# Feed-forward gate and up projections as seven block products in place of eight, with a six-place weight ring

## What is computed

```python
def swiglu(h, w_in, w_out):
    gt, up = jnp.split(h @ w_in, 2, axis=-1)       # w_in: 1024 x 5632
    return (jax.nn.silu(gt) * up) @ w_out          # w_out: 2816 x 1024
x = layer_norm(ALPHA * x + g1 * ox, ln_g[i, 0], ln_b[i, 0])
x = layer_norm(ALPHA * x + g2 * swiglu(x * (1.0 + sc2) + sh2, ...), ...)
```

## Time and profile before

| | us |
|---|---|
| median of 3 runs | 2932.16 (2931.82 to 2932.55) |
| the profiled execution: span from first to last instruction (no other time of it is given) | 2928.7 |
| TensorE busy | 2802.1 (96%) |
| VectorE / ScalarE / GpSimd busy | 1401.3 / 747.1 / 1211.0 |

### The profile page before, as it was taken

How to read it: one execution, slowest core, us unless ns; L and a number is a source line. 1 busy time by engine, 2 the same in 40 slices (tenths; PEclk the granted TensorE clock), 3 DMA queues, 4 the chain that set the end, 5 groups by cost and what they waited for, 6 DMA issues and landing times.

```text
span 2928.7 us, 38039 instructions
## 1 busy us (share of the span) xinstructions
PE 2802.1 (96%) x14458; PEld 2246.8 (77%) x14458; DVE 1401.3 (48%) x2147; ACT 747.1 (26%) x1218; POOL 1211.0 (41%) x583
## 2 busy tenths in 40 slices
PE   7899999999989899999997999999989999999997
PEld 2588888888867777777775888888778878888885
DVE  6433433334355466555556654645450045555555
ACT  3600000000034433333333222231441321222112
POOL 0544444444445321222221334433264366556555
PEclk9999999999999999999998999999999999999999
DMA  9211111111102010101010111112222311111113
GB/s 388 81 51 50 50 43 50 50 43 50 43 30 86 31 37 29 36 29 36 29 36 15 51 51 50 50 43 58 87 94 101 108 66 65 57 57 57 57 65 123
DMA packets 62900, 185.35 MB, mean 63 GB/s; under 512 B 17108, under 2 KB 23380, under 8 KB 60648
## 3 DMA queue, kind: packets, MB, share of 16 engines
q1 hardware_dynamic: 42016, 152.68, 15.3%
q10 hardware_dynamic: 20808, 31.61, 3.1%
HBM read 163.22 MB, written 21.05 MB: 63 GB/s over the span
## 4 chain that ended last, share of the span: by engine, by line
PE 86%; DVE 6%; ACT 3%; issue 3%; DMA 1%; POOL 1%; DVEq 0%; ACTq 0%; SPq 0%; POOLq 0%
PE ps L717 26%; PE ps L719 25%; PE ps L718 25%; PE ps L1057 2%; DVE acc L2197 1%; PE ps L785 1%; PE ps L1068 1%; DMA resid<-x_t 1%; PE ps L891 1%; PE ps L858 1%; PE ps L1414 1%; ACT sg_z L2000 1%; PE ps L1105 0%; PE ps L818 0%; DVE da_al L2368 0%
## 5 line engine op out<-in xcount | busy, mean ns | idle before, releaser
L540 POOL TENSOR_TENSOR slab_hi<-slab_raw,zero 128x1024 fp32r<-128x1024 f32 x227 | 446.4, 1967 | 1498.0 <-PE ps L719 1351.3
L717 PE MATMUL ps<-h_hi,slab_hi 128*128 128x512 f32 x2256 | 894.5, 397 | 12.5 <-POOL slab_lo L544 5.6
L718 PE MATMUL ps<-h_lo,slab_hi 128*128 128x512 f32 x2256 | 883.1, 391 | 0.0
L719 PE MATMUL ps<-h_hi,slab_lo 128*128 128x512 f32 x2256 | 883.1, 391 | 0.0
L544 POOL TENSOR_TENSOR slab_lo<-slab_raw,slab_hi 128x1024 fp32r<-128x1024 f32 x227 | 562.0, 2476 | 19.4 <-DVE mean L2251 1.7
L717 PEld LDWEIGHTS ps<-h_hi,slab_hi 128*128 128x128 f32 x2256 | 425.9, 189 | 112.6 <-issue 14.9
L719 PEld LDWEIGHTS ps<-h_hi,slab_lo 128*128 128x128 f32 x2256 | 425.6, 189 | 91.1
L718 PEld LDWEIGHTS ps<-h_lo,slab_hi 128*128 128x128 f32 x2256 | 426.0, 189 | 84.6
L2204 DVE TENSOR_TENSOR ffn_p<-ps,ffn_g 128x1024 f32<-128x1024 f32 x22 | 26.9, 1224 | 454.3 <-PE ps L719 448.7
L2197 DVE TENSOR_TENSOR acc<-ps,acc 128x512 f32<-128x512 f32 x352 | 228.2, 684 | 24.1 <-PE ps L719 22.9
L2195 DVE SCALAR_TENSOR_TENSOR resid<-ps,mod,resid 128x512 f32<-128x512 f32 x320 | 213.1, 743 | 0.0
(11 more groups left out here) (326 smaller groups left out, 4001.5 us busy)
## 6 DMA issues: line engine op xcount, KB each, us to landing
slab_raw<-w_in SPq DMA_DIRECT2D x168, 512.0 KB, 3.6
mod_big<-mod_w SPq DMA_DIRECT2D x12, 2048.0 KB, 11.7
slab_raw<-w_c SPq DMA_DIRECT2D x43, 512.0 KB, 3.6
res_scr<-resid ACTq DMA_DIRECT2D x4, 2048.0 KB, 7.2
resid<-res_scr ACTq DMA_DIRECT2D x2, 4096.0 KB, 12.3
gv_scr<-sg_t ACTq DMA_DIRECT2D x4, 2048.0 KB, 7.0
slab_raw<-gv_scr SPq DMA_DIRECT2D x16, 512.0 KB, 3.5
resid<-x_t SPq DMA_DIRECT2D x2, 2048.0 KB, 16.3
```

What stands on the lines that cost most here:

```text
L540: pool.tensor_tensor(hi, raw[slot][:], zeros, ALU.add).then_inc(hi_done.sem, 1)
L717: pe.matmul(dst, w_h, r_h, start=first, stop=False, skip_group_check=True)
L718: pe.matmul(dst, w_h, r_l, start=False, stop=False, skip_group_check=True)
L719: return pe.matmul(dst, w_l, r_h, start=False, stop=last, skip_group_check=True)
```

## The change

Per tile f = 1 to 21 the 2 x 2 product (gate, up) x (first, second half of k) times (first, second half of k) x (first, second half of the tokens) is made from seven block products (the Winograd form) in place of eight. A block product is 4 k x 3 = 12 matmuls over 512 tokens. Tile 0 stays as it was.

- Weights: of the four 128 x 512 blocks A11, A12 (gate), A21, A22 (up), GpSimd makes S1 = A21 + A22, S3 = A11 - A21, S2 = S1 - A11, S4 = A12 - S2 per tile (`weight_sums`). A11, S1, A12, S3, S4, S2, A22 and the two halves of w_out's slab then go, each as a high and a low part of 128 x 512, through a ring of six places (the three old slabs halved). All nine pairs are made on GpSimd.
- Inputs, once: four combinations T1 to T4 of h's four blocks, in float32, by GpSimd (T1) and VectorE (the rest); high parts on ScalarE, low parts on VectorE (12) and GpSimd (T3's four).
- Results: seven products in four banks (4 to 7), products accumulate in pairs where the sums allow it. ScalarE copies the first (`copy_first`) and the S1 product (`copy_fifth`) out of PSUM; VectorE makes four sums from PSUM and one from SBUF per tile, and the two products with the silu in halves.
- The residual's scaling by alpha moves from ScalarE to VectorE (`residual_in`). The output pass uses `PS[0]` and `PS[1]`, and waits for VectorE as before, four halves ahead.

```diff
 (GpSimd)
+def weight_sums(f):
+    for load in in_load: pool.wait_ge(load.sem, load.at(f))
+    a21 = block_source(S3)
+    pool.tensor_tensor(ffn_s1[:], a21, block_source(A22), ALU.add).then_inc(r_sum.sem, 1)
+    pool.wait_ge(r_sum.sem, r_sum.at(f, 0))
+    pool.tensor_tensor(a21, block_source(A11), a21, ALU.subtract).then_inc(r_sum.sem, 1)
+    pool.tensor_tensor(ffn_s2[:], ffn_s1[:], block_source(A11), ALU.subtract).then_inc(r_sum.sem, 1)
+    pool.wait_ge(r_sum.sem, r_sum.at(f, 2))
+    pool.tensor_tensor(ffn_s4[:], block_source(A12), ffn_s2[:], ALU.subtract).then_inc(r_sum.sem, 1)
+def ring_high(f, b, j):          # then block_high: wait for the sum or the load, 128x512 + zero
+    if j >= A22: pool.wait_ge(r_mm.sem, r_mm.at(f, j - A22))
+    elif j < S4: pool.wait_ge(r_mm.sem, r_mm.at(f - 1, j + 3))
+    else:        pool.wait_ge(f_om.sem, f_om.at(f - 2, (KT - 1, 2 * KT - 1)[j - S4]))
+def ring_turn(f, b):
+    for j in (A11, S1, A12, S3, S4, S2):
+        ring_high(f, b, j); block_low(f, b, j)
+    hidden_low(f - 1, 0)
+    for j in (A22, OUT_0, OUT_1):
+        ring_high(f, b, j); block_low(f, b, j)
+    weight_sums(f + 1)
+weight_sums(1)                   # the start, after h's low parts 1, 3, 5, 7
+for j in (A11, S1):
+    block_high(1, 0, j); block_low(1, 0, j)
+for k in range(2):
+    split_low(0, (KT + 2 * k + 1,)); input_difference(2 * k); input_difference(2 * k + 1)
+split_low(0, (2 * KT - 3, 2 * KT - 1))
 (TensorE)
+def ffn_in(f, b, first=False):
+    pe.wait_ge(f_silu.sem, f_silu.at(f - 1, 0));  ffn_product(f, b, A11)
+    pe.wait_ge(f_c.sem, f_c.at(f - 1, 0));        ffn_product(f, b, S1, (t_low, 0) if first else None)
+    pe.wait_ge(f_pc.sem, f_pc.at(f, 0));          ffn_product(f, b, A12)
+    pe.wait_ge(f_c.sem, f_c.at(f - 1, 2));        ffn_product(f, b, S3, (t3_low, 0) if first else None)
+    pe.wait_ge(f_pc.sem, f_pc.at(f, 1));          ffn_product(f, b, S4)
+    pe.wait_ge(f_u.sem, f_u.at(f - 1));           ffn_product(f, b, S2, (t_low, 4) if first else None)
+    pe.wait_ge(f_y.sem, f_y.at(f));               ffn_product(f, b, A22, (t_low, 8) if first else None)
 (VectorE)
+def ffn_upper(f):                # after product S3
+    dve.tensor_tensor(ffn_p5[:], BANK[7], ffn_p5[:], ALU.add)
+def ffn_hidden(f):               # after product S2, each with its waits
+    dve.tensor_tensor(ffn_u[:], BANK[5], ffn_p1[:], ALU.add)
+    dve.tensor_tensor(ffn_p1[:], BANK[6], ffn_u[:], ALU.add)
+    dve.tensor_tensor(ffn_p5[:], ffn_p5[:], ffn_u[:], ALU.add)
+    dve.tensor_tensor(ffn_c[:], BANK[7], ffn_u[:], ALU.add)        # after product A22
+    dve.tensor_tensor(ffn_c[:], ffn_c[:], ffn_g[:], ALU.mult)
+    dve.tensor_tensor(ffn_p5[:], ffn_p5[:], ffn_p1[:], ALU.mult)
+def ffn(f): ffn_upper(f); ffn_hidden(f); ffn_add_out(f - 1)
+# the start, in VectorE's order
+for k in half_k: turned_low(k, t1_lo[:, k, :], t1_raw[:, k, :], t1_hi[:, k, :])
+for k in half_k: input_fourth(k)
+for k in half_k: turned_low(KT + k, t2_lo[:, k, :], t2_raw[:, k, :], t2_hi[:, k, :])
+for k in half_k: turned_low(3 * KT // 2 + k, h_lo[:, k, HALF:T], t4_raw[:, k, :], h_hi[:, k, HALF:T])
+ffn_upper(1)
+dve.tensor_tensor(ffn_0[:], PS[1], ffn_0[:], ALU.mult)             # tile 0's hidden
+for k in range(KT): residual_in(k)                                # resid * ALPHA + res_b0, 128x1024
+ffn_hidden(1)
+ffn_add_out(0)
 (SP: slab 0 of f is loaded after the low part of A12 of f-1, slab 1 after A22's, slab C after OUT_1's)
```

More of the change, by code:

```diff
@@ L81, with ring_slot @@
 LAST_ON_POOL = KT + 5
+N_RING, N_BLOCKS, N_PROD = 6, 9, 7
+A11, S1, A12, S3, S4, S2, A22, OUT_0, OUT_1 = range(N_BLOCKS)
+LAST_F = F_TILES - 1
+FIRST_PAIR = IN_FFN_OUT - 2
+def ring_slot(b, j):
+    return (N_BLOCKS * b + j + 4) % N_RING
 DA_TILES = {3: (0, 1), 4: (2, 3), 5: (4, 5), 6: (6,), 7: (7,)}
@@ new lines, in _, with block_high @@
+            RING_SUM = {S1: 0, S3: 1, S2: 2, S4: 3}
+            def block_high(f, b, j):
+                if j in RING_SUM:
+                    pool.wait_ge(r_sum.sem, r_sum.at(f, RING_SUM[j]))
+                else:
+                    load, turn = {A11: (in_load[0], f), A12: (in_load[0], f), A22: (in_load[1], f)}.get(j, (c_load, f - 1))
+                    pool.wait_ge(load.sem, load.at(turn))
+                pool.tensor_tensor(ring(all_hi, b, j).rearrange("p k f -> p (k f)"), block_source(j), zero[:, 0:1].to_broadcast([P, HALF]), ALU.add)\
+                    .then_inc(r_hi.sem, 1)
@@ L601, in _ @@
+            ring_turn(2, 1)
+            with pool.Fori(1, F_TILES // 2 - 1) as j:
+                for b in range(2):
+                    ring_turn(2 * j + (1 + b), b)
+            for j in (A11, S1, A12, S3, S4, S2):
+                ring_high(LAST_F, 0, j)
+                block_low(LAST_F, 0, j)
+            hidden_low(LAST_F - 1, 0)
+            ring_high(LAST_F, 0, A22)
+            block_low(LAST_F, 0, A22)
             for s in range(2):
+                pool.wait_ge(r_mm.sem, r_mm.at(LAST_F, (S3, S2)[s]))
@@ new lines, in _, with ffn_product @@
+            FFN_OPENS = (A11, S1, S3, S2)
+            def ffn_product(f, b, j, ready=None):
+                pe.wait_ge(r_lo.sem, r_lo.at(f, j))
+                w_h, w_l = ring(all_hi, b, j), ring(all_lo, b, j)
+                r_h, r_l = FFN_INPUT[j]
+                for k in range(KT // 2):
+                    if ready is not None:
+                        pe.wait_ge(ready[0].sem, ready[0].at(ready[1] + k))
+                    mm = three(FFN_BANK[j], w_h[:, k, :], w_l[:, k, :], r_h[:, k, :], r_l[:, k, :],
+                               k == 0 and j in FFN_OPENS, k == KT // 2 - 1)
+                mm.then_inc(r_mm.sem, 1)
@@ new lines, in ffn_out @@
+            def ffn_out(f, b):
+                o = f - 1
+                pe.wait_ge(f_lo.sem, f_lo.at(o))
+                for d in range(KT):
+                    j = (OUT_0, OUT_1)[d // 4]
+                    if d % 4 == 0:
+                        pe.wait_ge(r_lo.sem, r_lo.at(f, j))
+                    for e in range(2):
+                        if d >= 2:
+                            pe.wait_ge(out_ev.sem, out_ev.at(o, 2 * (d - 2) + e))
+                        else:
+                            pe.wait_ge(out_ev.sem, out_ev.at(o - 1, 2 * (KT - 2 + d) + e))
+                        three(PS[d % 2][:, half_of(e)], ring(all_hi, b, j)[:, d % 4, :], ring(all_lo, b, j)[:, d % 4, :],
+                              ffn_hi0[:, half_of(e)], ffn_lo0[:, half_of(e)], True, True).then_inc(f_om.sem, 1)
```

376 lines of the change are left out of this document (294 added, 82 removed).

## The result

The changed kernel takes 2948.23 us (median of 4; 2944.26 to 2956.13), the kernel before beside it 2931.99 (2930.37 to 2932.55): ratio 1.0060, 95% interval 1.0047 to 1.0074. It is slower, by 16 us; I had forecast 2928, 4 us faster. 84 matmuls a tile went in as planned, and by their count 57 us of TensorE work are gone. What took their place is read in four views.

The account below looks back on a forecast made before the run. The prediction took the kernel as TensorE-bound. Start +24.0, 19 turns -24.7, last tile's products -2.7 and final passes -0.4 sum to -3.8: span 2924.9, time 2928 us, range 2909 to 2948.

Parts of the forecast that it names:

- What bounds the kernel, what goes: TensorE bounds it; 84 matmuls for 96 in tiles 1 to 21 save 2.72 us each, 57.2 if nothing else moved.
- GpSimd, 29.1 and 30.2 us a turn: GpSimd's work per feed-forward turn: 29.1 us alone, 30.2 with port delays; almost no slack, but not setting the turn.
- The shared port: GpSimd and VectorE instructions with two SBUF tensors wait for each other's whole instruction; +1.1 us of GpSimd work per turn.
- The start, +24: Before tile 2's products: making T1 to T4 and scaling residuals delays them from 170.5 to 194.6; bounds 18 to 31.
- The turn, 31.7: One feed-forward turn: 30.27 us plus a 1.20 stall before the first residual addition, 31.47; bounds 30.7 to 32.7, taken 31.7.
- the long branch: At the first silu product GpSimd takes the port first; products end at 21.66 and 23.36, turn 32.6 us.
- -24.7: Forecast gain of the 19 loop turns, in us: 19 x (33.0 - 31.7).
- Rival 3, the clock: TensorE's clock falls at each turn's stall, 1.7 us each, 19 x 1.7 = +32; time 2960; chance 0.05.
- The forecast's branch: VectorE's first silu product gets the port ahead of GpSimd's next high part; turn 31.2 to 32.1; chance 0.58.
- rivals 1 and 3: 1: GpSimd takes the port first, turn 32.6, time 2945, chance 0.24. 3: clock falls at each stall, 2960, chance 0.05.
- The end, -3.1: After the loop: last tile's products -2.7 us, final passes -0.4; all behind unchanged.
- The sum: Whole span: +24.0 - 24.7 - 2.7 - 0.4 = -3.8 us; span 2924.9, time 2928.

Follow-up runs that it names:

- e1_late: Changed kernel with VectorE's two silu products behind the sixteen residual additions instead of ahead of them; 2905.84 us, ratio 0.9909.
- e4_late_six: As e1_late, with product S3 cut to 3 matmuls in place of 12 (arithmetic left out); 2894.38 us, ratio 0.9873.
- the repetition: The changed kernel, unaltered, run once more on a second chip; 2964.66 us, ratio 1.0100.
- e9: Changed kernel with three small GpSimd memsets per tile added ahead of the four weight sums; 2930.44 us, ratio 0.9989.
- e3_res: Changed kernel with the eight residual scalings moved back from VectorE to ScalarE; 2955.91 us, ratio 1.0086.
- e7_dve_later: Changed kernel with one small VectorE memset added ahead of the first silu product; 2969.49 us, ratio 1.0114.
- e10: As e4_late_six, with product A12 also cut to three k of four, for a longer TensorE idle; 2897.06 us, ratio 0.9882.
- e6: Changed kernel with one small GpSimd memset per tile added ahead of the four weight sums; 2942.14 us, ratio 1.0026.

## Why the prediction was wrong, step by step

- **What bounds the kernel, what goes**: right. The seven products of a tile without a stall and its output pass measure 30.43 us (e1_late) where I had 30.27. Of the 0.16, 0.14 lie inside the seven products (19.21 from the first matmul to the output pass, 19.07 forecast), whose changes of bank and satisfied waits I had priced at nothing; it is small beside the rest.
- **GpSimd, 29.1 and 30.2 us a turn**: right. High parts 1.04, low parts 1.29, sums 1.29; 30.16 a turn with the port where nothing else binds (e4_late_six). The 29.4 of the windows are busy time, without the 0.08 behind each wait on an own result, and with the port.
- **The shared port**: right in kind and size. The rows at 443.68 and 409.46 show 0.69 and 1.53 for one order, 1.54 and 1.76 for the other; I had 0.7 and 1.5, 1.5 and 1.7.
- **The start, +24**: right. The upper addition of tile 2 follows its fourth product by 0.36, so the products began at 206.10 - 0.36 - 4 x 2.72 = 194.9; I had 194.6. VectorE's 16 instructions ran from 139.25 to 164.85 (139.3 to 165), TensorE stood 10.58 at 184.74.
- **The turn, 31.7: this step failed.** The chain's arithmetic gave both branches, 31.47 and 32.6, and both came, at 31.5 and 32.8 (31.47 with some luck: the turn without a stall is 0.16 longer than forecast, the stall 1.07 and not 1.20). What failed is the sentence that chose between them: "I take 31.7, since unlisted waits in fifteen GpSimd instructions can only make it later". It looked for lateness on GpSimd alone. GpSimd was on time, its next high part at 20.14 to 20.26 where I had the port free at 20.21. VectorE was late: inside the loop its first silu product starts 0.82 behind c and not 0.72, at 20.23 and not 20.15; only in the turn ahead of the loop does it start at 20.14. A term of 0.08 on VectorE was put at nothing, and the margin was 0.06. The margin was also too wide by my own rows: the next GpSimd instruction starts 0.05 before the last one's end, so 0.01 was left. Why the step from c is longer inside the loop no run shows. So 11 of 19 turns (16 of 19 in the repetition) took the long branch, and -24.7 became 19 x (32.63 - 33.01) = -7.3.
- **Rival 3, the clock, was priced too low.** I gave it 0.05 on the ground of one row, 1.69 us idle without a fall. Only the long branch makes an idle of 2 us, and behind that the clock fell in 5 of 11 turns, at 1.5 us each (34.3 against 32.8). The forecast's branch, with 0.8 to 1.0 idle, never lost it: 0 of 19 in e9, and 0 of the 26 short turns of the other profiles. So rivals 1 and 3 are not two cases but one: the second comes only with the first. The Trainium skill, "TensorE: Matmul & The Clock Gate", A second HAM failure mode, which I had set aside, describes for another kernel short idles between groups of matmuls at which the clock goes back and forth, paid for in throughput; these turns agree, with five falls in 19 turns at 1.5 us each.
- **The end, -3.1**: right. Tile 21's products begin 17.1 later than before (814.8, against the 797.7 that the turns of 33.01 give), and the stage's last addition comes at 867.16 in place of 853.11, 14.1 later: -3.0 between them. (826.67 - 819.5 is 7.2, where the prediction has 7.3; the slip is 0.1.)
- **The sum**: +24.4 - 7.3 - 3.0 = +14.1 at the end of the stage. The span grew by 18.0. The other 3.9 lie in the rest of the program, which is unchanged: 2079.5 us after the stage, 2075.6 before. In e3_res it took 2075.2 and in e7_dve_later 2082.0, with the same code. So 4 us are within what this part varies by from one profiled execution to another. It goes with the clock granted there: 0.984 before and in e3_res, 0.980 after, 0.979 in e7_dve_later. The whole kernel before varies in the same way, from 2925.06 at 0.989 to 2936.90 at 0.982 on the third chip. What sets that clock isn't shown.

Open: what makes the clock fall behind one idle of 2 us and not behind the next of the same length (in these kernels mostly where the turn before was long as well, but not so in e10), and how much of the difference between 2948 and 2965 is the chip and how much the execution. Unaltered, the changed kernel wasn't run on the third chip.

## What to carry to other kernels

When a sum comes out at two values with a margin below what you can read in durations, don't pick one: both can occur, and the forecast is the mixture, with whatever the worse one drags in. Count the unlisted waits of both engines in such a race, not of one. Take instructions off the path between the last product and the first release of a PSUM bank before you count what the saved matmuls bring; moving two products behind sixteen additions was worth 42 us here, where the seven-for-eight form by itself cost 16. And when two kernels that should be equal differ, repeat one of them unaltered before you explain the other (e3_res).

## What the hardware showed that I had not expected

- Work added to GpSimd, which was busy 29.4 us of a turn already, made the kernel faster, by 18 us against the changed kernel's first figure and by 34 against its second (e9), because 0.1 us decided which engine had the shared port first. Neither figure was taken on e9's chip, as far as the record names chips.
- The price of the wrong order at one place: 0.85 + 0.23 us on two products (1.54 - 0.69, 1.76 - 1.53), 1.1 of idle on TensorE, and in 3 of 9 (e6) to 17 of 18 (e7) cases 1.5 more for the clock.
- Idles of TensorE once a turn and the falls behind them: 0.87 to 0.98 us, none in 19 turns (e9); 1.58 us, none in 18 (e4); 1.94 to 2.05 us, 5 of 11, 14 of 16, 3 of 9, 17 of 18 (changed, again, e6, e7); 2.25 us, 6 of 12 (e10).
- Equal long turns lose the clock unequally: 42 of 45 behind another long turn, 8 of 23 behind a short one.
